# Two latent layers in stages of 256 tokens, or in one stage each by blocks of 128 tokens

## The reference

```
for i in range(2):
    h = modulate(rms_norm(x, norm1_gain[i]), sh1, sc1)          # 256 x 1024
    q, k, v = project_qkv(h, w_qkv[i], q_gain, k_gain, rope)    # 8 query heads, 2 key heads of 128
    o = global attention over 256 context + 256 latent keys (i = 0),
        or within a window of 128 tokens, the context and a sink (i = 1)
    x = x + g1 * (o @ w_o[i])
    h2 = modulate(rms_norm(x, norm2_gain[i]), sh2, sc2)
    # PEER: 8 heads, each picks 16 of 128 x 128 experts for each token
    s1, s2 = (h2 @ w_q) against 128 sub-keys each
    top 16 of each, top 16 of the 256 sums -> expert numbers, softmax weights g
    x = x + g2 * sum over 128 experts of g * gelu(u[expert] . h2) * v[expert]
```

## Time and profile before

| | us |
|---|---|
| three runs | 3165.12, 3167.58 (median), 3170.16 |
| span of the profiled execution | 3163.4 |
| last part of the first block (feed-forward of layer 1) | 1190 to 1428 |
| latent layer 0, up to the first gather | 1428 to 1620 |
| latent layer 0, gathers and experts | 1620 to 2286 |
| latent layer 1, up to the first gather | 2286 to 2494 |
| latent layer 1, gathers and experts | 2494 to 3154 |
| writing out | 3154 to 3163.4 |

### The profile page before, as it was taken

The page is one execution under the profiler, slowest core; times in us unless marked ns, Lnnn a source line. Parts: engine busy times, 40 slices in busy tenths (PEclk is TensorE's granted clock), DMA queues, the critical chain, the costliest instruction groups (busy, mean ns, idle before and its releaser), DMA issues.

```text
span 3163.4 us, 30793 instructions
## 1 busy us (share of the span) xinstructions
PE 2598.7 (82%) x10048; PEld 1719.6 (54%) x10048; DVE 2245.3 (71%) x5446; ACT 584.7 (18%) x1613; POOL 1215.8 (38%) x1028
## 2 busy tenths in 40 slices
PE   6798786899797679998898787777799987877776
PEld 2677664788675568886683332332367733333222
DVE  0438978699788877768778886665563698866555
ACT  2221212100021120002321111121214211111111
POOL 0002543466564355651434444444200254444441
PEclk8899898999898899999999999999999999999999
DMA  9327876799998489994779999999731599999997
GB/s 391 148 95 250 323 277 226 274 386 390 374 347 317 170 303 380 409 409 163 240 263 420 420 420 420 420 420 420 314 109 54 232 419 420 420 420 420 420 420 290
DMA packets 209521, 1029.22 MB, mean 325 GB/s; under 512 B 23409, under 2 KB 24945, under 8 KB 142929
## 3 DMA queue, kind: packets, MB, share of 16 engines
q0 software_dynamic: 147456, 805.37, 63.9%
q1 hardware_dynamic: 60624, 217.34, 18.2%
q10 hardware_dynamic: 1280, 4.54, 0.4%
HBM read 1021.98 MB, written 5.18 MB: 325 GB/s over the span
## 4 chain that ended last, share of the span: by engine, by line
DMA 35%; PE 35%; DVE 22%; issue 4%; ACT 1%; POOL 1%; SPq 1%; DVEq 0%; ACTq 0%; another core or an unknown queue 0%; POOLq 0%
DMA w_ring<-in_peer_uv,expert 11%; PE ps L2410 6%; DMA own<-in_peer_uv,expert 6%; DMA ctx_ring<-in_peer_uv,expert 5%; PE ps L2060 5%; DVE sum L1442 4%; PE ps L449 4%; PE ps L1172 4%; PE ps L1253 3%; DMA w_ring<-in_weights 3%; PE ps L1759 3%; DMA ctx_ring<-in_peer_v,ctx_expert 3%; DMA hT<-in_peer_uv,expert 2%; DMA low<-in_peer_uv,expert 2%; DVE ctx_ring L1445 1%
## 5 line engine op out<-in xcount | busy, mean ns | idle before, releaser
L2410 PE MATMUL ps<-w_ring,diag 128*128 128x512 f32 x876 | 425.6, 631 | 120.6 <-ACT diag L2355 120.6
L2410 PEld LDWEIGHTS ps<-w_ring,diag 128*128 128x128 f32 x876 | 167.2, 199 | 374.6 <-ACT diag L2355 194.6
L2197 DVE SCALAR_TENSOR_TENSOR w_ring<-w_ring,htok 128x1024 f32<-128x1024 f32 x219 | 267.7, 1223 | 138.9 <-DMA w_ring<-in_peer_uv,expert 137.7
L2249 POOL DMA_INDIRECT w_ring<-in_peer_uv,expert x219 | 240.7, 1099 | 312.7 <-PE ps L2410 269.2
L1253 PE MATMUL ps<-mix,w_ring 128*128 128x256 f32 x1408 | 307.5, 382 | 8.8 <-DVE mix L395 8.8
L1425 POOL DMA_INDIRECT ctx_ring<-in_peer_u,ctx_expert x126 | 160.1, 1270 | 399.3 <-DVEq L1992 247.8
L1253 PEld LDWEIGHTS ps<-mix,w_ring 128*128 128x128 f32 x1408 | 269.6, 192 | 46.7 <-issue 9.6
L2355 ACT ACTIVATE diag<-consts_sb 128x128 f32<-128x128 f32 x512 | 179.0, 394 | 614.2 <-DVE consts_sb L2290 592.8
L1425 POOL DMA_INDIRECT ctx_ring<-in_peer_v,ctx_expert x152 | 187.8, 1235 | 230.2 <-DVE sum L1442 144.8
L2249 POOL DMA_INDIRECT own<-in_peer_uv,expert x75 | 83.8, 1117 | 346.2 <-DVEq L1992 260.9
L2410 PE MATMUL ps<-ctx_ring,diag 128*128 128x512 f32 x296 | 142.8, 618 | 41.2 <-ACT diag L2355 41.2
(11 more groups left out here) (437 smaller groups left out, 5027.6 us busy)
## 6 DMA issues: line engine op xcount, KB each, us to landing
w_ring<-in_weights SPq DMA_DIRECT2D x392, 512.0 KB
w_ring<-in_peer_uv,expert POOLq DMA_INDIRECT x219, 24.4
ctx_ring<-in_peer_v,ctx_expert POOLq DMA_INDIRECT x152
ctx_ring<-in_peer_u,ctx_expert POOLq DMA_INDIRECT x126
ctx_more<-in_peer_v,ctx_expert POOLq DMA_INDIRECT x104
consts_sb<-in_consts SPq DMA_DIRECT2D x1, 1536.0 KB, 9.8
ctx_more<-in_peer_u,ctx_expert POOLq DMA_INDIRECT x80
own<-in_peer_uv,expert POOLq DMA_INDIRECT x75
```

What stands on the lines that cost most here:

```text
L2197: v.scalar_tensor_tensor(out=u, in0=u, scalar=1.0, in1=m.htok[:, e // SLOTS, :], op0=ALU.mult, op1=ALU.mult, accum_out=m.dots[:, e:e + 1]) ...
L2249: pool.indirect_dma_start(out=entry(e), out_offset=None, in_=table, in_offset=bass.IndirectOffsetOnAxis(ap=m.expert[:, blk, k:k + 1], axis ...
L2410: ins = pe.matmul(m.ps[:, 2 * blk + half, :], b.diag[:, e % DIAGS, :], entry(e)[:, D + half * 512:D + (half + 1) * 512], start=(k == 0), s ...
```

## The change

Both latent layers are written anew as one stage each, `latent_layer`, which works on blocks of 128 tokens and keeps the residual stream with tokens on partitions (`m.x`). `project_qkv`, `second_attention` and `peer_queries` remain for the context stream only (`project_context`, `context_attention`, `context_queries`). The order within a latent layer:

1. Products of keys and values and of queries (`made`): in layer 0 six items of 8 products 128 x 512 (two of keys and values, four of queries); in layer 1 three, since the other five (`coming`) were computed beside the entries of layer 0. Head norms are sums along the free axis; the rotary step is done on rows; TensorE turns the rows back.
2. Attention of block 0, its out projection, its norm, the first pair's queries and the routing of that pair whole; then the gathers may start.
3. Attention of block 1.
4. The 256 entries. Beside them (`beside(e)`, at fixed entry numbers) run the out projection of block 1, the other seven query groups and their routing, and in layer 0 the context stream's return and layer 1's first five items.

```diff
-STAGE_SEMS = 46
+STAGE_SEMS = 56
-LATENT_PARTS = PRELUDE[1:] + [(1, "w_qkv_2"), (1, "w_o_2"), (1, "peer_w_q_2")]
+LATENT_GROUPS = [("w_qkv_2", 2), ("w_qkv_2", 0), ("w_qkv_2", 1), ("w_o_2", 0), ("w_o_2", 1)] + [
+    ("peer_w_q_2", j) for j in range(NG_PQ)]
-WEIGH_AT = (3, 1)
+WEIGH_AT = (2, 1)
-                    rows.take(v, 4 if j < WEIGH_AT[l] else 3 + j % 2, "feed_forward")
+                    rows.take(v, 4, "feed_forward")
-    FIRST_SHARE = dict(in_projection=30, rwkv=48, attention=22, out_projection=16, feed_forward=110)
-    SECOND_SHARE = dict(in_projection=36, rwkv=50, attention=21, out_projection=17, feed_forward=114)
-    TAIL_SHARE = dict(project_qkv=8, attention=16, out_projection=14, peer_queries=10)
+    FIRST_SHARE = dict(in_projection=30, rwkv=50, attention=24, out_projection=16, feed_forward=106)
+    SECOND_SHARE = dict(in_projection=36, rwkv=50, attention=21, out_projection=17, feed_forward=127)
+    TAIL_SHARE = dict(latent=35)
```

The gates are written to device memory as rows and read back broadcast; the first time in the stage of the context's projection, behind the constants:

```diff
+def keep_gates(sp, m, i, kept):
+    for n, part in enumerate((G1, G2)):
+        sp.dma_start(m.kept_gates[i, n].rearrange("(k p) -> p k", p=P), m.mods[:, i, part:part + KT, LATENTS],
+                     allow_slow_non_contiguous=True).then_inc(kept, 16)
+    sp.wait_ge(kept, 32)
@@ project_context
+            sp.dma_start(m.c[:, LATE_AT:CONSTS.shape[1]], d.consts[:, LATE_AT:CONSTS.shape[1]]).then_inc(s.consts_in, 16)
+            keep_gates(sp, m, 0, s.gates_kept)
+            sp.wait_ge(s.consts_in, 16)
```

The places and the fixed entry numbers:

```diff
-ENTRIES = 15
-OWN = 2
+OWN = 4
+SEQUENCE = ((0, 0), (0, 1), (0, 2), (1, 0), (0, 3), (1, 1), (1, 2), (1, 3))
+QUERY_AT = {1: 4, 2: 14, 3: 28, 4: 42, 5: 58, 6: 74, 7: 90}
+ROUTE_AT = {1: (14, 1), 2: (24, 2), 3: (44, 2), 4: (64, 2), 5: (84, 3), 6: (111, 3), 7: (145, 3)}
+X1_AT = 3
+MODS_AT, SUMS_AT, CONTEXT_AT = 106, 108, 116
+HTOK_AT = 124
+X0_AT = 130
+NEXT_AT = 140
@@ latent_layer
+        opened = {f"own{j}": (0, None) for j in range(OWN)}
+        if i:
+            opened.update(ring0=(0, None), ring1=(0, None), stream=(0, None), sums=(0, None),
+                          keys=(12, (s.o_done, 2 * PAIRS)), queries=(12, wide.filled(("out", 1, 1))))
+            for j in range(1, NG_PQ):
+                slot = ring.slot_of[g0 + G_PQ + j]
+                for half in range(2):
+                    opened[f"group{2 * slot + half}"] = (QUERY_AT[PLACE_OF[1, j]] + 14, wide.filled(("pq", 1, j)))
+        else:
+            opened.update(ring0=(0, (m.ctx_used, TT * 2 * SLOTS)), ring1=(0, (m.ctx_used, TT * 2 * SLOTS)),
+                          stream=(0, turned.filled(("x", 1, 1))),
+                          sums=(SUMS_AT + 12, turned.filled(("sums", KT // 2 - 1))))
```

So layer 0 has 7 places up to entry 119 and 8 from entry 120; layer 1 has 8, 10 from entry 12, and up to 16 later. SyncE, VectorE and TensorE (shortened to the order of the work):

```diff
+        @block.sync
+            ring.load_to(sp, g0 + G_PQ + 3, g0, group_done)
+            if between:
+                sp.wait_ge(*wide.filled(("out", 1, 1)))
+                sp.dma_start(m.cT[:, :, :], m.kept_c).then_inc(s.stream_in, 16)
+            sp.wait_ge(s.x_added, added(("h2", 1)))
+            load_gate(1)
+            ring.load_to(sp, g0 + NG_LATENT + (3 if between else 0), g0, group_done)
...
+        @block.vector
+            for n in range(len(made)):
+                item_rows(n)
+                if not i:
+                    rows.take(v, 3, "latent")
+            attend(0, None if i else lambda h: rows.take(v, 2, "latent"))
+            if not i:
+                rows.take_rest(v, "latent")
+            for half in range(2):
+                add_out(0, half)
+            norm_rows(("h2", 0))
+            norm_first_half(("h2", 0))
+            for at in range(Route.STEPS):
+                route_step(0, at)
+            routes[0].shift(0, PAIR)
+            attend(1)
+            routes[0].weights(0, PAIR, 0, 0)
+            for e in range(TOTAL):
+                dot(e)
+                n = e // BATCH
+                if e % BATCH == 0 and n:
+                    weigh(n - 1)
+                if e % BATCH == BATCH - 1:
+                    gelu_argument(n)
+                beside(e)
...
+        @block.tensor
+            def beside(e):
+                if e < 4:
+                    out_part(1, e // 2, 4 * (e % 2), 4 * (e % 2) + 4)
+                if e == X1_AT + 6:
+                    norm_turn(("h2", 1))
+                for n, at in QUERY_AT.items():
+                    if at <= e < at + 4:
+                        query_part(n, 2 * (e - at), 2 * (e - at) + 2)
+                    if e == at + 5:
+                        query_turn(n)
+                    if e == at + 7:
+                        query_scores(n)
+            for e in range(TOTAL):
+                beside(e)
+                pe.wait_ge(s.built, e + 1)
+                for half in range(2):
+                    ins = pe.matmul(m.ps[:, 2 * blk + half, :], m.diag[:, e % DIAGS, :],
+                                    entry(e)[:, D + half * 512:D + (half + 1) * 512], ...)
+                ins.then_inc(s.used, 1)
```

More of the change, by code:

```diff
@@ new lines @@
+ENTRY_PLACES = [f"own{j}" for j in range(OWN)] + ["ring0", "ring1", "stream", "sums", "keys", "queries"] + [
+    f"group{j}" for j in range(2 * WSLOTS)]
+SEQUENCE = ((0, 0), (0, 1), (0, 2), (1, 0), (0, 3), (1, 1), (1, 2), (1, 3))
+PLACE_OF = {bg: n for n, bg in enumerate(SEQUENCE)}
+QUERY_AT = {1: 4, 2: 14, 3: 28, 4: 42, 5: 58, 6: 74, 7: 90}
+ROUTE_AT = {1: (14, 1), 2: (24, 2), 3: (44, 2), 4: (64, 2), 5: (84, 3), 6: (111, 3), 7: (145, 3)}
+X1_AT = 3
+MODS_AT, SUMS_AT, CONTEXT_AT = 106, 108, 116
@@ new lines, with __init__ @@
+class EntryPlaces:
+    def __init__(self, m, i, opened):
+        self.m = m
+        last = {}
+        self.place, self.before, self.turn = [], [], []
+        for e in range(TT * SLOTS):
+            free = [name for name in opened if opened[name][0] <= e]
+            name = min(free, key=lambda name: (last.get(name, opened[name][0] - 8), ENTRY_PLACES.index(name)))
+            self.place.append(name)
+            self.before.append((None, last[name] + 1) if name in last else opened[name][1])
+            last[name] = e
+            m.entries_landed[name] += 16
+            self.turn.append(m.entries_landed[name])
+    def of(self, e):
+        m, name = self.m, self.place[e]
+        if name.startswith("own"):
+            return m.own[:, int(name[3:]), :]
+        if name.startswith("ring"):
+            j = int(name[4:])
+            return m.ctx_ring[:, 2 * j:2 * j + 2, :].rearrange("p s n -> p (s n)")
+        if name == "stream":
+            return m.xT[:, :, :].rearrange("p k t -> p (k t)")
+        if name == "sums":
+            return m.low[:, 3 * D:5 * D]
+        if name == "keys":
+            return m.low[:, D:3 * D]
+        if name == "queries":
+            return m.qT[:, :, :].rearrange("p k t -> p (k t)")
+        j = int(name[5:])
+        return m.w[:, j // 2, 2 * D * (j % 2):2 * D * (j % 2 + 1)]
+    def landed(self, e):
+        return self.m.entry_in[self.place[e]], self.turn[e]
@@ L2308, in context_back @@
[L2308 to L2314 removed]
+                v.sem_inc(wide.release("mods"), 1)
+                v.sem_inc(s.gains_made, 1)
@@ L2481 @@
+            latent_layer(nc, m, d, ring, i, LATENT_AT + NG_LATENT * i, rows)
 def kernel(**inputs):
```

1108 lines of the change are left out of this document (742 added, 366 removed).

## The result

The changed kernel takes 3185.64 us (median of 5 runs, 3184.47 to 3192.78), the kernel before 3167.58: a ratio of 1.0062 with a 95% interval of 1.0044 to 1.0080. Timed again on another occasion it was 1.0056 (1.0040 to 1.0072). It is slower by 0.6%, 18 to 20 us; the forecast was 12 us faster. The profiled execution has a span of 3183.2 us against 3163.4.

The account below looks back on a forecast made before the run. Gathering the entries was taken as memory-bound, with 192 and 208 us stretches before them where DMA was not busy. Terms summed to -12 us: span 3151, median 3155, against 3163.4 (span) before; range 3095 to 3220.

Parts of the forecast that it names:

- First block, +12: Stages before the latent layers: second feed-forward +17, first one -10, rows given to rwkv and attention +5; +12 us.
- Gates, +6: End of the context's projection stage: two gate writes, 2048 pieces of 4 bytes, go behind the constants; +6 us.
- Front 0, 149: Layer 0 from stage start to the entries' start: 192 to 149 us, -43.
- the passage on the clock: TensorE's clock falls at waits; attention of block 1 wholly at the lower level would cost +18 a layer, span 3187.
- Start of the entries, 110: Both layers, first gather to entry 21's reissue: 110 us from TensorE's owed work, +29 and +39 over before.
- The rest of layer 0, +35: Layer 0's other 234 entries: weight groups sharing the full queue +20, fewer places +15.
- fewer places +15: Layer 0's entries: 7 places instead of 13, most queries starve the DMA by 1 to 2 us; +15 us.
- Weights at +20: Layer 0's entries: last query group and three groups of layer 1, 4 x 2.1 MB at 420 GB/s; +20 us.
- Front 1, 112: Layer 1 before its entries, stage change to first pair's routing: 208 to 112 us, -96.
- the rest of layer 1, +10: Layer 1's other 234 entries: one weight group +5, fewer places (10 from entry 12) +5.
- too few places: Rival, layer 0's entries 22 to 255: longer rounds cost 0.25 us an entry, 59 there, total 3209; chance 0.22.
- small writes: Rival: gate writes take 36 us instead of 6 in the context's stage, more amid the full queue; 3200; chance 0.10.

Follow-up runs that it names:

- the run of light weights: Changed kernel with loads of the next layer's first three weight groups beside layer 0's entries cut to a sixteenth: 1.0020 to the kernel before.
- gates, items and places mended: Changed kernel with gates written in 512-byte pieces, VectorE's item work two entries later, two more places in layer 0: 0.9930 to the kernel before, 3146.8 us.

## Why the prediction was wrong

The direction was wrong; the reading of the fronts was not. Step by step:

- **First block, +12, measured +22.** The terms ahead of it came out near: the second feed-forward's first weight issue is 0.8 us later than before (1202.64 for 1201.85), of 7.5 that the gates had cost, so the shifted rows of the first feed-forward and the stages around it gave 6.7 where I had 5. The +17 of the second feed-forward was the mis-sized term. I took its 13 rows at DMA bytes, 1.3 us each; they cost 29 us in all, 2.2 each. They are taken after TensorE's last product. From 1417 to 1434 the queue is full at 409 GB/s, half of it (3.45 of 6.96 MB) the latent stage's weights, and a row comes every 2.56 us. I had the row for this price, 2.56 us at the end of the first feed-forward, and used it only for the rows that went.
- **Gates, +6, measured +7.5 in the context's stage** (153.24 for 145.74 at TensorE's next product; 5.6 in the other profile of the changed kernel). Near, and in part by luck: 6 was picked between 2 and 36, and the row read as a small write is one of 256 KB. The same writes amid layer 0's entries I charged nothing for, though the rival on them did. They take 4 to 7 us there.
- **Front 0, 149, measured 158.** The steps in TensorE's timeline of the changed kernel, with the stage's start at 1457.6 (first scores, first output product, first query product):

```profile
1516.75 3.12 PE L2373 MATMUL ps<-low,qT 128*128 128x512 f32 x4
...
1562.61 14.48 PE L2333 MATMUL ps<-w_ring,qT 128*128 128x512 f32 x32 [0.47 <-ACT qT L2614]
...
1586.23 9.43 PE L2333 MATMUL ps<-w_ring,hT 128*128 128x512 f32 x16 [1.64 <-issue]
```

  The items end on R+59 (forecast 58). The attention ends on R+105 for 97; waits for the landings of its context rows are 6.1 us of the 8. The queries take 9.43 us instead of 6.87, the granted clock being 0.74 from 1576 to 1596, as the passage on the clock had feared for a place; the routing takes 15.4 for 15.5. The attention of block 1, behind it, starts at the lower level as that passage said (0.52 granted from 1612 to 1622) and leaves it soon (0.84 from 1615 to 1636, 0.92 from 1616 to 1650), so the 18 us a layer that it weighed did not come.
- **Start of the entries, 110, measured 104 and 101.** Near; the bound named (TensorE's owed products) is the right one: TensorE is busy for 90.1 of the 100 us from 1620 to 1720. How much the seven places add to it is not shown. The kernel before needs 91 from its first gather with seven places where it needed 81, but two places more, from entry 12 on, took only 2 from the changed kernel's 104.
- **The rest of layer 0, +35, measured +63.** This is the step that failed, and in it the term "fewer places +15". Weights at +20 were sized well (fifteen sixteenths of three of the four groups, 14 us at that price, gave back 11 to 13). The argument on places was: round 17.5 us, 3.3 left over, lateness of 1 to 2 us in bursts. Alone, in the kernel before, seven places cost 36 us in layer 0 (10 up to entry 21's product, 26 in the rest) and 45 in layer 1. With two more for part of the way, 10 to 12 came back in the changed kernel. The slack of 3.3 was taken from means and from a transfer into idle queues, 5.3 us. In rotation a gather takes 8.6 (the run of light weights, from 1750 to 1900). That stretch takes 57.6 MB, 55 entries, in 150 us, so a round of seven is about 19 us (an estimate), of which some 10.5 lie between landing and reissue, where I had 8.9. Nothing of the 3.3 is left. That late places come in company, as the two of a batch do, would explain it and is not shown. Beside it stand 12 to 14 us that no term had: VectorE's five waits for the items' roots. I had costed the items' operations and not what they wait for. With gates, items and places mended the rest of layer 0 stands at +35, the very figure of the forecast; that is the weights' 20 with what is left of all the others, and no support for +15 as the price of seven places.
- **Front 1, 112, measured 117.5; the rest of layer 1, +10, measured +1; end, -4, measured -3.7.** Right within 9. With ten places from entry 12 on, layer 1 loses next to nothing after its start.

Of the rivals, "too few places" was the right mechanism with a price that was too high (59 in layer 0, where seven places alone cost the kernel before 36); "small writes" was real with a price that was too high (36 in the context's stage, where 7.5 were measured). My sign for the first one was a bad instrument: "DMA share above 0.95, or 0.90 if places fail". My signs for places (DMA below 0.9) and for small writes (the attention stage at 160) both stayed away, and both causes were there. The share stayed at 0.96 in layer 0 and 1.00 in the window from 1750 to 1900, while the rate fell to 376 and 399. By the share alone the places would have been acquitted.

On the small writes the Trainium skill ("DMA: Bandwidth & Descriptors", Specifications) has pieces under 512 bytes done as read-modify-write. The traces agree so far that 4 KB in 4-byte pieces land after 16.1 us and the 1.5 MB ahead of them 5 us later than before, and that with pieces of 512 bytes the 1.5 MB take 9.8 us again; whether by that mechanism, no run here shows.

Open: how the 36 us of seven places, the weights, the items' waits and the writes divide layer 0's 87 us (753 for 666) exactly, since each was measured with the others present or absent altogether; and why rows cost 2 us in every stage tried. The price was measured at the end of the feed-forward, in front 0 and in the stages ahead; only its waits and its 1.28 us of work were read from a trace, not what would shorten them.

## What to carry to other kernels

When a queue is kept full by a few places in rotation, judge it by GB/s and not by busy share, and size the number of places by trying it in the kernel as it is, before the work is moved: 13 to 10 cost layer 0 only 3 us here, 8 to 7 cost more than 10 to 8. Work put beside a full stream has a price by what it waits for, beside that of its own operations; ask for a result only when its producer, which is some entries behind, can have it. A forecast that moves work between stages needs the price at the place of arrival: a row counted at its bytes, 1.3 us, cost 2 or more wherever it was put.

## What the runs showed that was not expected

- DMA share 1.00 at 399 GB/s with seven places, 1.01 at 419 with nine, with much the same work beside them, and 1.06 at 111 GB/s for 10 us while the small writes go out: here the share does not say how much is moved.
- The step of one place from eight to seven (678 to 702 us of entries in layer 0) costs more than twice that of two places from ten to eight (669 to 678).
- 2048 writes of 4 bytes, 8 KB in all, lower the whole rate for 10 us from about 400 to 111 GB/s.
